# First expert products of a PEER layer: one 512-column matmul for both parts of x, slabs of 256 experts with all 1024 rows

## Chip, cores and metric

The kernel runs on one core of one Trainium2 chip. The metric is the device time of one execution in microseconds. Three executions of the kernel before took 1482.37 (median), 1482.51 and 1480.81 us.

## The reference, cut to what matters

Two transformer blocks follow one another on 256 tokens of width 1024 (float32). The change sits in the last operation, the PEER layer of the second block:

```python
def peer(h, w_q, sub_keys, expert_u, expert_v):      # h: (1, 256, 1024)
    q = einsum('bsd,dq->bsq', h, w_q)                # 8 heads x 2 x 128
    scores = einsum('bshpc,hpnc->bshpn', q, sub_keys)
    top_s, top_i = top_k(scores, 16)
    ...                                              # 256 candidates, the best 16 per head, softmax: gate, best_i
    u = take(expert_u, best_i)                       # expert_u, expert_v: (16384, 1024)
    act = gelu(einsum('td,tkd->tk', x, u), approximate=False)
    v = take(expert_v, best_i)
    return einsum('tk,tkd->td', gate * act, v)
```

The kernel gathers nothing: it computes x times all 16384 rows of expert_u, applies gelu, multiplies by a dense table of gates (zero where an expert wasn't chosen), and multiplies by all of expert_v.

## The kernel before, in words

**Slabs.** All large weights come in 207 slabs of 1 MB (128 partitions x 2048 float32), numbered in order of use. Four slots hold them. For each slab n the sync engine's queue (SP) issues the load once VectorE is done with slab n-4 (`load`, L295 to L300). ScalarE copies the slab to a rounded fp32r high part once TensorE is done with slab n-4 (`hi`, L986 to L992). VectorE subtracts, which gives the low part (`lo`, L1348 to L1353). TensorE takes slab n when both are there (`take`) and signals with `used`. A product of float32 quality is three fp32r matmuls (`mm3`, L417): high x high, high x low, low x high. All matmuls are issued from L412, so rows name them by their tiles.

**Stages of the PEER layer.** Slabs 71 to 78 are query weights, 79 to 142 are expert_u (S_EU, 64 slabs), 143 to 206 are expert_v (S_EV, 64 slabs). In what follows "U slab s" is slab 79+s. Two U slabs make one chunk c of 512 experts: the first holds rows 0 to 511 of the model width for these 512 experts, the second rows 512 to 1023. `feature_half` (L887) runs 4 groups of 128 experts x 4 blocks of 128 rows, three matmuls of 256 tokens each: 48 matmuls per slab, with the weights stationary and x moving. The sums of a chunk fill two PSUM banks (0 and 1 for even c, 2 and 3 for odd c). After the second slab ScalarE applies gelu straight from PSUM to `hidden_out` (L1313 to L1318), SP stores it to HBM (L372 to L376), and TensorE may use the banks for chunk c+2 (L944).

**Side work in the U stage.** VectorE's program is one hand-written sequence. Between its `lo(next(slab))` calls it does the top-k work (`choose`, four calls with six slabs each, L1772), then the keys of the chosen experts (`chosen_keys`), and from U slab 32 on the gate table: 32 gate steps of 16 compares each (`gate_step`, L1899), one or two per slab in turn (`gates_due`, L93). TensorE multiplies what each step made (`gate_step`, L928), into banks 4 to 7, ScalarE copies it (`copy_gates`), and SP stores every four steps (L377). Before the first gate step VectorE waits until ScalarE has copied three transposed selections, the last of which TensorE makes after U slab 31 (L1921, L951, L1327). The order of VectorE around that wait is:

```python
            DVE.wait_ge(*after("choice_copied", 3))
            for n in slab:
                lo(n)
                s = n - S_EU - 4
                for i in range(gates_due(s + 1), gates_due(s + 2)):
                    gate_step(i)
```

**Into the V stage.** SP runs ahead. After the load of slab 142 it issues `load_weighted` for c = 0, 1, 2 (two loads of 512 KB each, hidden values and gates, L383 to L387), then slabs 143 and 144, then the store of hidden chunk 28, slabs 145 and 146, the store of chunk 29, and so on, all in one queue. Their source lines are:

```python
                if n == S_EV - 1:
                    for k in range(2):
                        SP.wait_ge(*after(f"gates_stored{k}", 16 * (S // GATE_T // 2)))
                    for c in range(3):
                        load_weighted(c)
```

VectorE multiplies hidden values by gates (`weigh`, L1914), ScalarE rounds (`weighted_hi`, L1309), VectorE subtracts (`weighted_low`, L1918), and TensorE multiplies with expert_v in matmuls of 512 columns.

Of the kernel before, what the change touches and what calls it, by code (L numbers as in the profile page):

```python
# [6 lines left out]
P = 128  # L7
S = 256
# [134 lines left out]
def program(nc, a, out):  # L143
# [5 lines left out]
    with ctx:  # L149
# [7 lines left out]
        xh = sb("x_hi", [P, KT, S], f32r)  # L157
        xl = sb("x_lo", [P, KT, S], f32r)
# [129 lines left out]
        w_lo = [wl[:], xl[:, 0:EX_A], xl[:, EX_A:2 * EX_A]]  # L288
        hidden_store = nc.dram_tensor("hidden_store", (EX_N, P, EX_A * S), f32).ap()
# [3 lines left out]
        def sync_program():  # L293

            def load(n):  # L295
                name, j = slabs[n]
                if n >= NSLOT:
                    SP.wait_ge(lo_made[n % NSLOT], n // NSLOT)
                src = a[name].rearrange("n p m -> (n p) m")[j * P:j * P + P, :]
                SP.dma_start(raw[:, n % NSLOT, :], src).then_inc(raw_loaded[n % NSLOT], 16)  # L300
# [68 lines left out]
            for n in range(S_PQ + 2, S_END):  # L369
# [39 lines left out]
        def tensor_program():  # L409
# [548 lines left out]
            for c in range(EX_N):  # L958
# [16 lines left out]
                if c == 1:  # L975
                    PE.wait_ge(*after("gate2_diagonal_made", 1))
                    PE.wait_ge(*after("hidden_made", EX_N))
                    for half in range(2):
                        ins = mm(ps[:, half, :], ones[:], carve(1024, TB, 512)[:, half, :])
                    ins.then_inc(sem("gate2_spread"), 1)  # L980

        def scalar_program():
# [3 lines left out]
            def hi(*numbers):  # L986
                for n in numbers:
                    slot = n % NSLOT
                    ACTE.wait_ge(raw_loaded[slot], 16 * (n // NSLOT + 1))
# [320 lines left out]

            for s in range(2 * EX_N):
                c, half = divmod(s, 2)
                if half:  # L1313
                    if c >= 2:
                        ACTE.wait_ge(*after(f"hidden_stored{c % 2}", 16 * (c // 2)))
                    slab_done(ACTE, S_EU + s)
                    ACTE.activation(hidden_out[c % 2], banks(2 * (c % 2), 2).rearrange("p (a t) -> p a t", a=EX_A),  # L1317
                                    ACT.Gelu).then_inc(sem("hidden_made"), 1)  # L1318
# [11 lines left out]
                if s == 2 * EX_N - 3:  # L1330
                    weighted_hi(0)

# [10 lines left out]
        def vector_program():  # L1343
# [427 lines left out]

            def choose(c):  # L1772
# [8 lines left out]
                lo(next(slab))  # L1781
# [4 lines left out]
                lo(next(slab))  # L1786
# [8 lines left out]
                lo(next(slab))  # L1795
# [3 lines left out]
                lo(next(slab))  # L1799
# [14 lines left out]
                lo(next(slab))  # L1814
# [8 lines left out]
                lo(next(slab))  # L1823
# [5 lines left out]
            for _ in range(5):  # L1829
                lo(next(slab))  # L1830
# [15 lines left out]
            lo(next(slab))  # L1846
# [12 lines left out]
            lo(next(slab))  # L1859
# [12 lines left out]
            lo(next(slab))  # L1872

            def chosen_keys(src, m, dst, tb):
# [6 lines left out]
                lo(next(slab))  # L1881
# [8 lines left out]
            lo(next(slab))  # L1890
            chosen_keys(of_i, 0, sa, 1).then_inc(sem("first_keys_made"), 1)
            lo(next(slab))
            V(chosen_keys(of_j, 1, sbb, 0))
            lo(next(slab))
            chosen_keys(of_j, 1, sbb, 1).then_inc(sem("second_keys_made"), 1)
            lo(next(slab))


            def gate_step(i):  # L1899
                n, t0 = i % 2, 8 * i  # L1900
                if i >= 2:
                    DVE.wait_ge(*after("hits_used", 2 * (i - 2) + 2))
                for j in range(8):
# [18 lines left out]
            for n in slab:  # L1922
                lo(n)
# [10 lines left out]
            lo(next(slab))  # L1934
# [103 lines left out]
```

## Time and profile before

| | |
|---|---|
| three executions | 1480.81, 1482.37, 1482.51 us |
| the profiled execution | 1480.88 us, span of its instructions 1479.6 us |
| TensorE busy | 1393.1 us (94%) |
| VectorE busy | 967.1 us (65%) |
| ScalarE busy | 623.9 us (42%) |
| DMA queue of SP | 316 MB, 59.4% of 16 engines |
| mean granted clock of TensorE | 0.965 |

Busy times are sums over the span. A timeline lists each instruction with its start, its duration and the idle time of its engine before it, with what released it. Matmuls overlap in the pipeline, so the time that one costs is the distance between two starts, not its duration. "Landing" of a DMA is the time from its issue to its completion signal.

### The profile page before, as it was taken

The page shows a single profiled execution, that of the slowest core. Times are in us where ns is not written, and L with a number is a line of the kernel's source. Part 1 is how long each engine was busy: PE and PEld are TensorE (multiplying, and loading weights), DVE is VectorE, ACT ScalarE, POOL GpSimd, SP SyncE. Part 2 cuts the span into 40 slices and gives each one's busy share as a digit, 9 for nine tenths or more (in the row PEclk, how much of TensorE's full clock was granted, in tenths as well). Part 3 has the DMA queues.
Part 4 walks back from the last instruction along what each step waited for, and adds up shares of the span by engine and source line. Part 5 has one row for each costly group of instructions (what it writes and reads, how often), then busy time and mean ns, then how long its engine had stood idle before and what let it go on. Part 6 is the DMA issues. An engine that isn't in the chain of part 4 may idle for free.

```text
span 1479.6 us, 19658 instructions
## 1 busy us (share of the span) xinstructions
PE 1393.1 (94%) x8262; PEld 1230.3 (83%) x8262; DVE 967.1 (65%) x1527; ACT 623.9 (42%) x534; POOL 35.1 (2%) x31
## 2 busy tenths in 40 slices
PE   4897968999999999799999999999999999999998
PEld 3786747888888988699999999999997777777776
DVE  4453645888736684748887879899446565655654
ACT  4344434443424853344434444444444434344341
POOL 0010010000002010000000000000000000000000
PEclk9999979999989998899999999999999999999999
DMA  7440316899724311436676748878887777777660
GB/s 292 153 169 3 114 42 273 320 381 377 276 73 185 115 57 58 190 123 214 217 235 225 240 156 270 264 247 256 270 321 279 281 257 271 278 280 277 257 256 29
DMA packets 83239, 317.39 MB, mean 215 GB/s; under 512 B 6096, under 2 KB 40144, under 8 KB 53200
## 3 DMA queue, kind: packets, MB, share of 16 engines
q1 hardware_dynamic: 83152, 316.14, 59.4%
q8 instruction: 65, 1.06, 0.3%
q14 instruction: 22, 0.18, 0.0%
HBM read 281.51 MB, written 34.60 MB: 214 GB/s over the span
## 4 chain that ended last, share of the span: by engine, by line
PE 81%; DVE 11%; ACT 7%; issue 1%; DMA 0%; POOL 0%; ACTq 0%; POOLq 0%
PE psum L412 78%; DVE slab_lo L1352 5%; ACT slab_hi L992 4%; PE psum L415 2%; DVE arena L1914 1%; DVE x_lo L1918 1%; ACT arena L1083 0%; DVE weighted_lo L1918 0%; ACT x_hi L1006 0%; DVE residual L1418 0%; ACT arena L995 0%; DMA arena<-in_mem 0%; DVE arena L1391 0%; DVE arena L1389 0%; ACT x_hi L1309 0%
## 5 line engine op out<-in xcount | busy, mean ns | idle before, releaser
L1352 DVE TENSOR_TENSOR slab_lo<-slab_raw,slab_hi 128x2048 fp32r<-128x2048 f32 x207 | 471.9, 2289 | 284.0 <-ACT slab_hi L992 274.5
L992 ACT ACTIVATE slab_hi<-slab_raw 128x2048 fp32r<-128x2048 f32 x207 | 393.6, 1909 | 273.2 <-PE psum L412 273.2
L412 PE MATMUL psum<-x_hi,slab_hi 128*128 128x256 f32 x1216 | 348.3, 286 | 3.7 <-ACT x_hi L1006 2.7
L412 PE MATMUL psum<-x_lo,slab_hi 128*128 128x256 f32 x1216 | 345.1, 284 | 0.0
L412 PE MATMUL psum<-x_hi,slab_lo 128*128 128x256 f32 x1216 | 345.0, 284 | 0.0
L412 PE MATMUL psum<-slab_hi,x_hi 128*128 128x512 f32 x768 | 311.0, 405 | 31.6 <-DVE slab_lo L1352 11.5
L412 PE MATMUL psum<-slab_lo,x_hi 128*128 128x512 f32 x768 | 304.7, 397 | 0.0
L412 PE MATMUL psum<-slab_hi,x_lo 128*128 128x512 f32 x768 | 304.5, 396 | 0.0
L412 PEld LDWEIGHTS psum<-x_hi,slab_hi 128*128 128x128 f32 x1216 | 234.4, 193 | 4.8 <-issue 3.1
L412 PEld LDWEIGHTS psum<-x_lo,slab_hi 128*128 128x128 f32 x1216 | 234.5, 193 | 0.0
L412 PEld LDWEIGHTS psum<-x_hi,slab_lo 128*128 128x128 f32 x1216 | 234.3, 193 | 0.0
L412 PEld LDWEIGHTS psum<-slab_hi,x_hi 128*128 128x128 f32 x768 | 148.1, 193 | 72.4 <-DVE x_lo L1918 16.1
L412 PEld LDWEIGHTS psum<-slab_hi,x_lo 128*128 128x128 f32 x768 | 147.5, 192 | 31.9
L412 PEld LDWEIGHTS psum<-slab_lo,x_hi 128*128 128x128 f32 x768 | 147.9, 193 | 29.9 <-issue 0.2
L412 PE MATMUL psum<-slab_hi,weighted_hi 128*128 128x512 f32 x280 | 111.7, 399 | 4.9 <-DVE weighted_lo L1918 2.9
L412 PE MATMUL psum<-slab_lo,weighted_hi 128*128 128x512 f32 x280 | 109.9, 392 | 0.0
L412 PE MATMUL psum<-slab_hi,weighted_lo 128*128 128x512 f32 x280 | 109.7, 392 | 0.0
L1906 DVE TENSOR_SCALAR arena<-iota,selected_first_keys,selected_gates 128x128 f32<-128x128 f32 x256 | 87.9, 343 | 0.0
L1317 ACT ACTIVATE arena<-psum 128x1024 f32<-128x1024 f32 x32 | 32.8, 1026 | 127.4 <-PE psum L412 127.4
L412 PEld LDWEIGHTS psum<-slab_hi,weighted_hi 128*128 128x128 f32 x280 | 52.9, 189 | 19.8 <-DVE weighted_lo L1918 7.7
L415 PE MATMUL psum<-ident,arena 128*128 128x128 f32 (+3 forms) x240 | 37.5, 312 | 30.2 <-DVE arena L1371 14.6
L412 PEld LDWEIGHTS psum<-slab_hi,weighted_lo 128*128 128x128 f32 x280 | 53.0, 189 | 11.3
(233 smaller groups left out, 1215.7 us busy)
## 6 DMA issues: line engine op xcount, KB each, us to landing
slab_raw<-in_ex_u SPq DMA_DIRECT2D x64, 1024.0 KB, 5.9
slab_raw<-in_ex_v SPq DMA_DIRECT2D x64, 1024.0 KB, 5.7
arena<-in_w_ada SPq DMA_DIRECT2D x24, 1024.0 KB, 6.9
slab_raw<-in_w_in SPq DMA_DIRECT2D x22, 1024.0 KB, 5.4
slab_raw<-in_w_gu SPq DMA_DIRECT2D x22, 1024.0 KB, 7.2
hidden_store<-arena SPq DMA_DIRECT2D x32, 512.0 KB, 6.9
gates_store<-arena SPq DMA_DIRECT2D x8, 2048.0 KB, 9.7
arena<-hidden_store SPq DMA_DIRECT2D x32, 512.0 KB, 5.8
```

Of the source, the lines that this page charges most:

```text
L412: return PE.matmul(out, lhsT, rhs, start=start, stop=stop)
L415: return PE.transpose(out, in_, ident[0:in_.shape[0], 0:in_.shape[0]])
L992: ACTE.activation(slab_hi[:, slot, :], raw[:, slot, :], ACT.Copy).then_inc(hi_made[slot], 1)
L1317: ACTE.activation(hidden_out[c % 2], banks(2 * (c % 2), 2).rearrange("p (a t) -> p a t", a=EX_A), ACT.Gelu).then_inc(sem("hidden_made"), 1)
L1352: DVE.tensor_tensor(slab_lo[:, slot, :], raw[:, slot, :], slab_hi[:, slot, :].bitcast(f32), ALU.subtract).then_inc(lo_made[slot], 1)
L1906: ins = DVE.tensor_scalar(gated[n][:, j, :], iota[:], sel_a[:, t], sel_g[:, t], ALU.is_equal, ALU.mult)
L1914: DVE.tensor_tensor(w4, w4, gates_in[n], ALU.mult).then_inc(sem("weighted_made"), 1)
L1918: DVE.tensor_tensor(w_lo[c % 3], hidden_in[c % 3], w_hi[c % 3].bitcast(f32), ALU.subtract).then_inc(sem("weighted_lo"), 1)
```

## The change

The two U slabs of a chunk are cut the other way: each slab now holds 256 experts with all 1024 rows. Its load is two DMAs that pick 1 KB pieces (256 float32) out of two of the old slabs. x_hi and x_lo become one tile `x_parts`, so that one matmul of 512 columns multiplies a high block of weights with both parts of x: the left half of a bank collects high x high and, by a second matmul of 256 columns, low x high; the right half collects high x low. After each slab ScalarE copies the right halves to a scratch tile (`hidden_low`), VectorE adds them to the left halves into `hidden_out` (`expert_sum`), and gelu runs in place one chunk later. TensorE reuses a pair of banks every second slab and waits for the sum. The store of hidden chunk c-2 must have landed before the sum of the first slab of chunk c; before, gelu of chunk c waited for it. Before the three first `load_weighted` SP waits for the 60th sum, because the scratch tile lies where they land.

```diff
-        xh = sb("x_hi", [P, KT, S], f32r)
-        xl = sb("x_lo", [P, KT, S], f32r)
+        xx = sb("x_parts", [P, 2, KT, S], f32r)
+        xh, xl = xx[:, 0], xx[:, 1]
...
+        LAST_HIT = 2 * EX_N - 4
+        def hidden_low(s):
+            flat = wf[:] if s < GATE_FROM else zs[:] if s >= LAST_HIT else carve(10240, 1024)
+            return flat[:, (s % 2) * 512:(s % 2) * 512 + 512].rearrange("p (a t) -> p a t", a=2)
...
+                if name == "ex_u":
+                    c, q = divmod(j, 2)
+                    src = a[name].rearrange("n p (k m) -> n p k m", k=4)[:, :, :, q * S:q * S + S]
+                    for half in range(2):
+                        SP.dma_start(raw[:, n % NSLOT, :].rearrange("p (k n) -> p k n", k=KT)[:, 4 * half:4 * half + 4, :], src[2 * c + half]).then_inc(
+                            raw_loaded[n % NSLOT], 16)
...
                 if n == S_EV - 1:
                     for k in range(2):
                         SP.wait_ge(*after(f"gates_stored{k}", 16 * (S // GATE_T // 2)))
+                    SP.wait_ge(*after("hidden_summed", LAST_HIT))
                     for c in range(3):
                         load_weighted(c)
...
+            def expert_half(bank, n):
+                take(n)
+                bh, bl = parts(n % NSLOT, KT, S)
+                for m in range(2):
+                    col = slice(m * P, m * P + P)
+                    for k in range(KT):
+                        mm(ps[:, bank + m, :], bh[:, k, col], xx[:, :, k, :], k == 0, False)
+                        ins = mm(ps[:, bank + m, 0:S], bl[:, k, col], xh[:, k, :], False, k == KT - 1)
+                used(ins, n)
+
             for s in range(2 * EX_N):
-                c, half = divmod(s, 2)
-                if half == 0:
-                    if c < 2:
-                        PE.wait_ge(*after("query_copied", 3 + c))
-                    else:
-                        PE.wait_ge(*after("hidden_made", c - 1))
-                feature_half(2 * (c % 2), S_EU + s, half)
+                if s < 2:
+                    PE.wait_ge(*after("query_copied", 3 + s))
+                else:
+                    PE.wait_ge(*after("hidden_summed", s - 1))
+                expert_half(2 * (s % 2), S_EU + s)
...
+            def hidden_gelu(c):
+                ACTE.wait_ge(*after("hidden_summed", 2 * c + 2))
+                ACTE.activation(hidden_out[c % 2], hidden_out[c % 2], ACT.Gelu).then_inc(sem("hidden_made"), 1)
+
             for s in range(2 * EX_N):
                 c, half = divmod(s, 2)
+                slab_done(ACTE, S_EU + s)
+                if s >= 2:
+                    ACTE.wait_ge(*after("hidden_summed", s - 1))
+                ACTE.activation(hidden_low(s), ps[:, 2 * half:2 * half + 2, S:2 * S], ACT.Copy).then_inc(
+                    sem("hidden_low_copied"), 1)
                 if half:
-                    ...
-                    ACTE.activation(hidden_out[c % 2], banks(2 * (c % 2), 2).rearrange("p (a t) -> p a t", a=EX_A),
-                                    ACT.Gelu).then_inc(sem("hidden_made"), 1)
+                    if c:
+                        hidden_gelu(c - 1)
                 hi(S_EU + s + 4)
...
+            hidden_gelu(EX_N - 1)
...
+            def expert_sum(s):
+                c, q = divmod(s, 2)
+                DVE.wait_ge(*after("hidden_low_copied", s + 1))
+                if q == 0 and c >= 2:
+                    DVE.wait_ge(*after(f"hidden_stored{c % 2}", 16 * (c // 2)))
+                DVE.tensor_tensor(hidden_out[c % 2][:, 2 * q:2 * q + 2, :], ps[:, 2 * q:2 * q + 2, 0:S], hidden_low(s),
+                                  ALU.add).then_inc(sem("hidden_summed"), 1)
+
+            def prepare(n):
+                s = n - S_EU - NSLOT
+                if 0 <= s < 2 * EX_N:
+                    expert_sum(s)
+                lo(n)
```

Every `lo(next(slab))` from slab 73 on becomes `prepare(next(slab))`, and `lo(n)` in the gate loop `prepare(n)`. So the sum of U slab s stands right before the low part of U slab s+4. `hi` waits for both DMAs of a U slab, and the wait at L977 is for all 64 sums.

## Rows read from the trace of the kernel before

**Rows 1.** Windows view: columns are wall, PE, PEld, DVE, ACT, POOL, PEclk, DMA share, GB/s
```profile
640.00:860.00 220.00, 220.00 (x1841) 220.00 (x1841) 166.75 (x479) 96.12 (x66) 0.00 (x0) 1.00 0.64 218
868.61:1038.95 170.34, 170.20 (x1452) 170.16 (x1453) 159.30 (x518) 74.92 (x61) 0.00 (x0) 1.00 0.79 246
1116.62:1474.00 357.38, 347.60 (x1492) 277.83 (x1492) 206.82 (x122) 140.98 (x90) 0.00 (x0) 1.00 0.66 247
```
**Rows 2.** Timeline of PE in the U stage: matmuls 0 and 43 of a row
```profile
799.82 0.28 PE L412 MATMUL psum<-x_hi,slab_lo 128*128 128x256 f32 x1
...
804.98 0.28 PE L412 MATMUL psum<-x_hi,slab_hi 128*128 128x256 f32 x1
```
**Rows 3.** Timeline of PE elsewhere: matmuls 0 and 17 of a row, 512 columns
```profile
459.69 0.39 PE L412 MATMUL psum<-slab_hi,x_hi 128*128 128x512 f32 x1
...
463.54 0.39 PE L412 MATMUL psum<-slab_hi,x_lo 128*128 128x512 f32 x1
```
**Rows 4.** Groups by shape, DVE and ACT: busy us, mean ns
```profile
L1387 DVE TENSOR_TENSOR arena<-psum,columns 128x512 f32<-128x512 f32 x16 | 10.5, 685 | 21.4 <-PE psum L415 21.4
L1648 DVE TENSOR_TENSOR arena<-arena,psum 128x768 f32<-128x768 f32 x4 | 3.8, 950 | 6.0 <-PE psum L412 6.0
L1136 ACT ACTIVATE hidden<-psum 128x512 f32<-128x512 f32 x11 | 6.6, 600 | 36.7 <-PE psum L412 36.7
```
**Rows 5.** Windows view: one choose cycle of 6 slabs, then one gate cycle of 2
```profile
746.90:781.46 34.56, 34.56 (x291) 34.56 (x289) 28.65 (x107) 14.23 (x9) 0.00 (x0) 1.00 0.69 227
941.28:958.15 16.87, 16.87 (x146) 16.87 (x145) 15.37 (x52) 7.48 (x6) 0.00 (x0) 1.00 0.73 238
```
**Rows 6.** Timeline of DVE at its longest gap between two low parts
```profile
751.91 2.27 DVE L1352 TENSOR_TENSOR slab_lo<-slab_raw,slab_hi 128x2048 fp32r<-128x2048 f32 x1
...
758.42 2.29 DVE L1352 TENSOR_TENSOR slab_lo<-slab_raw,slab_hi 128x2048 fp32r<-128x2048 f32 x1 [0.39 <-ACT slab_hi L992]
```
**Rows 7.** Timeline of ACT after U slab 31
```profile
859.66 1.03 ACT L1317 ACTIVATE arena<-psum 128x1024 f32<-128x1024 f32 x1 [3.84 <-PE psum L412]
860.58 1.91 ACT L992 ACTIVATE slab_hi<-slab_raw 128x2048 fp32r<-128x2048 f32 x1
862.38 0.38 ACT L1327 ACTIVATE selected_second_keys<-psum 128x256 f32<-128x256 f32 x1
```
**Rows 8.** Timeline of DVE after U slab 31: low parts of U slabs 34 to 36
```profile
862.79 2.29 DVE L1352 TENSOR_TENSOR slab_lo<-slab_raw,slab_hi 128x2048 fp32r<-128x2048 f32 x1 [9.50 <-ACT selected_second_keys L1327]
868.61 2.29 DVE L1352 TENSOR_TENSOR slab_lo<-slab_raw,slab_hi 128x2048 fp32r<-128x2048 f32 x1
878.06 2.29 DVE L1352 TENSOR_TENSOR slab_lo<-slab_raw,slab_hi 128x2048 fp32r<-128x2048 f32 x1
```
**Rows 9.** Timeline of PE: start of U slab 34
```profile
879.11 0.36 PE L412 MATMUL psum<-x_hi,slab_hi 128*128 128x256 f32 x1
```
**Rows 10.** Timeline of SP before the V stage
```profile
1063.40 0.89 SPq L375 DMA_DIRECT2D hidden_store<-arena  x1
1064.40 0.36 SPq L364 DMA_DIRECT2D arena<-hidden_store  x1
...
1074.55 0.33 SPq L300 DMA_DIRECT2D slab_raw<-in_ex_v  x1
1074.92 0.43 SPq L375 DMA_DIRECT2D hidden_store<-arena  x1
```
**Rows 11.** DMA view, issued between 1071 and 1076 us: x, KB, us to landing
```profile
hidden_store<-arena SPq DMA_DIRECT2D x1, 512.0 KB, 11.6
```
**Rows 12.** DMA view, issued between 690 and 860 us
```profile
hidden_store<-arena SPq DMA_DIRECT2D x15, 512.0 KB, 6.8
```
**Rows 13.** Windows view of 2 us in that burst
```profile
1074.00:1076.00 2.00, 2.00 (x19) 2.00 (x18) 0.52 (x1) 0.88 (x1) 0.00 (x0) 1.00 1.03 420
```
**Rows 14.** Timeline of PE: first matmuls of V chunk 0 and V chunk 1
```profile
1103.66 0.45 PE L412 MATMUL psum<-slab_hi,weighted_hi 128*128 128x512 f32 x1
...
1116.62 0.50 PE L412 MATMUL psum<-slab_hi,x_hi 128*128 128x512 f32 x1 [1.82 <-DVE x_lo L1918]
```
**Rows 15.** DMA issues of the page: stores made of 512 B pieces
```profile
gates_store<-arena SPq DMA_DIRECT2D x8, 2048.0 KB, 9.7
```

More of the change, by code:

```diff
@@ L288, in program, with transfers @@
         w_lo = [wl[:], xl[:, 0:EX_A], xl[:, EX_A:2 * EX_A]]
+        def transfers(n):
+            return sum(32 if S_EU <= m < S_EV else 16 for m in range(n % NSLOT, n + 1, NSLOT))
+        LAST_HIT = 2 * EX_N - 4
+        def hidden_low(s):
+            flat = wf[:] if s < GATE_FROM else zs[:] if s >= LAST_HIT else carve(10240, 1024)
+            return flat[:, (s % 2) * 512:(s % 2) * 512 + 512].rearrange("p (a t) -> p a t", a=2)
         hidden_store = nc.dram_tensor("hidden_store", (EX_N, P, EX_A * S), f32).ap()
@@ L988, in hi @@
                     slot = n % NSLOT
-                    ACTE.wait_ge(raw_loaded[slot], 16 * (n // NSLOT + 1))
+                    ACTE.wait_ge(raw_loaded[slot], transfers(n))
                     if n >= NSLOT:
@@ L1780, in choose @@
                     V(DVE.max_index(U(i16[:, 0:8]), v16[:, 0:8], values))
-                lo(next(slab))
+                prepare(next(slab))
                 for values, v16, i16 in rows[4:8]:
@@ L1785, in choose @@
                     V(DVE.match_replace(values, v16[:, 0:8], values, NEG))
-                lo(next(slab))
+                prepare(next(slab))
                 V.after()
@@ L1794, in choose @@
                     V(DVE.max(v16[:, 8:16], values))
-                lo(next(slab))
+                prepare(next(slab))
                 V.after()
@@ L1798, in choose @@
                     V(DVE.max_index(U(i16[:, 8:16]), v16[:, 8:16], values))
-                lo(next(slab))
+                prepare(next(slab))
                 V.after()
@@ L1813, in choose @@
                     V(DVE.max(v16[:, 0:8], values))
-                lo(next(slab))
+                prepare(next(slab))
                 V.after()
@@ L1822, in choose @@
                     V(DVE.max(v16[:, 8:16], values))
-                lo(next(slab))
+                prepare(next(slab))
                 V.after()
@@ L1829, in vector_program @@
             for _ in range(5):
-                lo(next(slab))
+                prepare(next(slab))
             choose(0)
@@ L1845, in vector_program @@
                 sem("gate_differences_made"), 1)
-            lo(next(slab))
+            prepare(next(slab))
             V.after()
@@ L1858, in vector_program @@
             V(DVE.tensor_tensor(of_j, mid, low_2, ALU.add))
-            lo(next(slab))
+            prepare(next(slab))
             DVE.wait_ge(*after("gate_exp_made", 1))
@@ L1871, in vector_program @@
             shape = [P, PEER_H, TOPK, TOPK]
-            lo(next(slab))
+            prepare(next(slab))
             def chosen_keys(src, m, dst, tb):
@@ L1880, in chosen_keys @@
                 V(DVE.tensor_tensor(key, hit, tfh[:, :, m, :].unsqueeze(3).to_broadcast(shape), ALU.mult))
-                lo(next(slab))
+                prepare(next(slab))
                 for half in (8, 4, 2):
@@ L1889, in vector_program @@
             V(chosen_keys(of_i, 0, sa, 0))
-            lo(next(slab))
+            prepare(next(slab))
             chosen_keys(of_i, 0, sa, 1).then_inc(sem("first_keys_made"), 1)
-            lo(next(slab))
+            prepare(next(slab))
             V(chosen_keys(of_j, 1, sbb, 0))
-            lo(next(slab))
+            prepare(next(slab))
             chosen_keys(of_j, 1, sbb, 1).then_inc(sem("second_keys_made"), 1)
-            lo(next(slab))
+            prepare(next(slab))
             def gate_step(i):
@@ L1902, in gate_step @@
                     DVE.wait_ge(*after("hits_used", 2 * (i - 2) + 2))
+                if i == 1:
+                    DVE.wait_ge(*after("hidden_summed", GATE_FROM))
                 for j in range(8):
@@ L1922, in vector_program @@
             for n in slab:
-                lo(n)
+                prepare(n)
                 s = n - S_EU - 4
@@ L1931, in vector_program @@
                     break
-            lo(next(slab))
+            prepare(next(slab))
             for c in range(EX_N):
```

10 lines of the change are left out of this document (4 added, 6 removed).

## The prediction

> **What bounds the kernel now.** I read the windows first, because the share of busy time (94% for TensorE) says nothing of where a stage is bound. From 640 to 860 us TensorE is busy all the time, VectorE 76% of it; in the gate stretch from 868.6 to 1039 us TensorE is again never idle, but VectorE is busy 159 of 170 us; in the V stage TensorE is at 97% [rows 1]. The granted clock is 1.00, the 2.4 GHz level, in all three, so no clock stands to be won. The U stage is therefore bound by TensorE's issue, with VectorE close behind in its second half. Next the timeline of TensorE, for the distance between starts: 43 matmuls of 256 columns take 5.16 us, 120 ns each [rows 2]; 17 of 512 columns take 3.85 us, 226.5 ns each [rows 3]. 256 more columns cost 106.5 ns, so each matmul costs some 13.4 ns beside its columns. Last the timelines of VectorE, ScalarE and SP, at the three places where the new waits fall: between two low parts, at U slab 31, and at the way into the V stage.
>
> **TensorE's part.** A U slab was 48 x 120 ns = 5.76 us. It becomes 16 x (226.5 + 120) = 5.55 us: the columns are the same, 16 matmuls fewer. That is 0.21 us per slab where TensorE is the bound. What it is worth is read stretch by stretch, since the change adds a sum to VectorE and ties TensorE to it: U slab s may start only when sum s-2 is made, one slab of time after U slab s-2 ended. The trace has no mixed row of 512 and 256 columns and none whose moving operand lies in two pieces; the bounds are 333 ns (both at the column rate) and 360 ns for the pair (no gain at all), and I take 346.5 from the two rows that have these shapes.
>
> A sentence of the skill speaks against the change here: the Trainium skill, "TensorE: Matmul & The Clock Gate", section "Wait — 56ns, not 53.3ns?", puts the fixed cost of a matmul at the full clock at about 2.5 ns beside its columns, for which the whole U stage would gain some 1024 x 2.5 ns = 2.6 us (an estimate from that page) and not 13.7. The trace doesn't agree: it shows 13.4 ns in both shapes [rows 2, 3].
>
> **The prices on the other engines.** The sum reads 128x512 from PSUM; such an operation takes 0.69 us, or some 0.60 us where the next one overlaps its end, as the low parts do (2.29 us long, 2.20 apart) [rows 4, 6]. I take 0.60; the ends are 0.60 and 0.95 (the 768-column row). The copy of the right halves takes 0.60 us on ScalarE [rows 4], which is busy 14.2 of 34.6 us [rows 5] and has the room. Gelu moves, 1.03 us as before [rows 7]. If ScalarE were full, each slab would pay these 0.6 us.
>
> **U slabs 0 to 31.** One choose cycle is six slabs: VectorE works 28.65 of 34.56 us [rows 5]. After: 28.65 + 6 x 0.60 = 32.3 us against 6 x 5.55 = 33.3 us. TensorE stays the bound, narrowly. The longest stretch between two low parts is 6.51 - 0.39 = 6.1 us [rows 6], 6.7 with a sum; a sum may be late by 4 us (a slab less copy and sum), so single long stretches are absorbed, except the first (the same work between the low parts of U slabs 4 and 5, when VectorE comes late out of the queries), where I count 0.6 us. The sum of an even slab also waits for the store of two chunks ago. Gelu now comes 1.9 us after the end of an odd slab; the store follows at once in an otherwise empty queue. Behind a slab load a store lands 6.8 us after issue [rows 12], of which 2.5 us are the slab at 420 GB/s [rows 13]; so alone some 4.7 us. It lands 6.6 us after the slab's end, and VectorE comes to that sum after some 8.6. Cost nothing; cover 2 us. Gain: 32 x 0.21 - 0.6 = 6.2 us.
>
> **U slabs 32 and 33.** VectorE waits for the third selection and now holds sum 30 behind that wait, so TensorE can't start U slab 32. ScalarE starts 0.25 us after slab 31's end (859.4): copy 0.5, gelu 1.0, high part 1.8, selection 0.4: VectorE starts at +3.95 (before: 862.79, +3.4) [rows 7, 8], TensorE at +4.7 instead of about +0.4. VectorE then goes from there to the end of gate step 2 in 878.06 - 862.79 = 15.27 us plus two sums [rows 8], to +20.4; the second half of TensorE's step 2 ends at +21.4, where U slab 34 started at +19.7 before [rows 9]. Cost 1.7 us.
>
> **U slabs 34 to 53.** A cycle of two slabs and three gate steps was 16.87 us with 15.37 us of VectorE [rows 5]. TensorE would need 16.44, VectorE needs 15.37 + 1.2 = 16.6 us: VectorE becomes the bound. Nine cycles gain 9 x 0.27 = 2.4 us, slabs 52 and 53 (one step each) 0.4 us. With a sum of 0.75 us the gain is gone. **U slabs 54 to 59** have no side work: 6 x 0.21 = 1.3 us.
>
> **Into the V stage.** Count from the end of U slab 59. Before, SP issued the three pairs of weighted loads at 1064.40, some 16 us ahead of that point, slab 144 at 1074.55, the store of chunk 28 at 1074.92, and that landed 11.6 us later, at 1086.5 [rows 10, 11]; gelu 30 needed it only at 1092. Now SP waits for sum 59, at +1.45. Behind it stand six 512 KB loads, two slabs and the store of chunk 28: 5.8 MB, 13.7 us at 420 GB/s [rows 13]. With the 3.4 us of fixed time that rows 12 leave (0.4 + 6.8 - 3.75 us of transfer) the store lands at +18.6. Sum 60 waits for it, and so does U slab 62, which would start at +11.1 and starts at +19.3. U slab 63 ends at +30.4. From there to V chunk 1 it was 12.96 us (1116.62 - 1103.66) [rows 14], through ScalarE's high part and VectorE's two low parts; the copy adds 0.5. V chunk 1 starts at +43.8; before, at 1116.62 - (1103.66 - 4 x 5.76) = +36.0. Cost 7.8 us, with the four slabs' gain in it. The V stage then runs as it did: its stalls come from the order of ScalarE and VectorE in each chunk and are not made up. Ends: 1074.92 + 11.6 - 1064.4 = 22.1 us for the same burst with older transfers ahead of it (3.5 us more cost), and 2.9 us of cost if only slab 143 is late (landing +14, and so sum 61, which stands behind its low part).
>
> **DMA.** A U load becomes 1024 pieces of 1 KB. A gates store moves 4096 pieces of 512 B in 9.7 us to landing [rows 15], so 1024 pieces take at most a quarter of it, 2.4 us, if the number of pieces counts, and half of it, 4.9 us, if the bytes do. Between 2.4 and 4.9 I take 3.0, near the bytes' rate in rows 13. A load is issued some 15 us before its use; cost nothing. Without that cover the gate stretch (share 0.79 [rows 1]) would be where it shows.
>
> **Sum.** 6.2 - 1.7 + 2.4 + 0.4 + 1.3 - 7.8 = 0.8 us faster: 1480.1 for the profiled execution of 1480.88 (span 1479.6). That execution is 1.5 us below the median of 1482.37; on the median's scale it is 1481.6. About 0.2%, 3 us, is what a measurement of this kernel can tell from no change.
>
> **Rivals.** (1) **The burst isn't in the way**: the store lands before its 5.2 MB of forerunners are through. Against it: in rows 11 it waited its turn. Then the last term is 2.9, the sum 5.7, the time 1476.7. (2) **VectorE becomes the bound of the whole U stage.** It decides from 0.75 us for a sum (rows 5: (33.3 - 28.65) / 6 and (16.87 - 15.37) / 2). At 0.95 us a choose cycle is 34.35, 1.1 over TensorE's, four times: 4.3 us lost; a gate cycle is 17.27, so 3.6 lost and not 2.4 won. Time 1481.6 + 4.3 + 6.0 = 1491.9. For it: VectorE's work in the gate stretch is 94%; against: its waits release within 0.05 us of ScalarE's end. (3) **The change doesn't save what it says**: the pair stays near 360 ns. Lost are 6.8, 2.4, 1.7 and 0.9 us: 1493.4. By the fixed cost of 2.5 ns as a mechanism of this kernel a slab saves 0.04 us and not 0.21; the same terms shrink to a fifth or less, 1490.9. That is the rule of the page named above, which rows 2 and 3 speak against. (4) **1 KB pieces fill the queues**: at 5.9 us of all 16 engines per slab, twice my value, a gate slab of 8.3 us has 5.9 + 2.7 for its share of a gates store + 0.6: 0.9 us too much, over 20 slabs 18 us: 1499.
>
> **How the numbers follow.** The forecast, within 3 us of no change: 0.38. Rival 1 and a milder burst: 0.24. Rival 2, with the burst's upper end: 0.23. Rival 3: 0.07 (of which 0.02 for the page's value), rival 4: 0.06. Some 0.02 is left for a gain that I don't see. Faster 0.26, within 0.2% 0.38, slower 0.36. The range reaches from rival 1 with a bit of the other ends, 1475.5, to a little short of rival 2's full price, 1490.5.
>
> **What the profile after would show.** 512 and 256 columns in turn, 346 ns a pair, and 5.55 us per slab up to U slab 31; TensorE idle for 4 us before U slab 32; VectorE without idle time in the gate stretch and a cycle of 16.6 us; one stall of about 8 us before U slab 62, released by a sum that waited for the store of chunk 28. I am wrong if that stall is missing, if TensorE waits for sums all through the choose cycles, or if loads of U slabs release ScalarE.

## The result, and the profile after

The changed kernel takes 1489.13 us, the median of 5 runs (1488.25 to 1489.67), against 1481.48 us for the kernel before (5 runs, 1480.81 to 1482.51). The ratio is 1.0045 with an interval of [1.0032, 1.0057]: slower by 7.65 us. The forecast was no change (1481.6); the time lies within the range, just short of its upper end of 1490.5. The profiled execution took 1489.13, its span is 1487.7 us. Page of the kernel after: its first part, then its queue, then the U loads and the stores:

```profile
PE 1388.5 (93%) x7238; PEld 1177.9 (79%) x7238; DVE 1004.5 (68%) x1591; ACT 656.7 (44%) x598; POOL 35.1 (2%) x31
...
q1 hardware_dynamic: 141520, 316.14, 59.8%
...
slab_raw<-in_ex_u SPq DMA_DIRECT2D x128, 512.0 KB, 5.3
...
hidden_store<-arena SPq DMA_DIRECT2D x32, 512.0 KB, 3.1
```

TensorE's share fell from 94% to 93%. U loads in 1 KB pieces land in 5.3 us (median), a store of the hidden values, now alone in the queue, in 3.1 (the forecast had 4.7 for it). None of this says where 8 us went. For that I cut both traces at the same events: ScalarE's first instruction after the end of a slab, which comes 0.25 us behind TensorE (gelu or the high part before [rows 7], the copy of the right halves after).

| stretch | before, us | after, us | change | forecast |
|---|---|---|---|---|
| end of U slab 0 to U slab 31 | 680.68 to 859.66: 178.98 | 680.20 to 856.56: 176.36 | -2.6 | -6.2 (slab 0 among them) |
| U slab 31 to 34 | to 885.21: 25.55 | to 885.80: 29.24 | +3.7 | +1.7, and slab 34's part |
| U slab 34 to 52 | to 1037.01: 151.80 | to 1034.52: 148.72 | -3.1 | -2.4 |
| U slab 52 to 59 | to 1080.88: 43.87 | to 1077.56: 43.04 | -0.8 | -1.7 |
| U slab 59 to start of V chunk 1 | to 1116.62: 35.74 | to 1124.51: 46.95 | +11.2 | +7.8 |
| V chunk 1 to the end | to 1479.6: 362.98 | to 1487.7: 363.2 | +0.2 | 0 |

With the 0.5 us by which slab 0 ended earlier, the changes add up to +8.1 us, the difference of the two spans. Those 0.5 us say nothing: slab 0 ends between 679.3 and 683.2 us in the ten profiles of this study, although the change and the edits leave alone what stands ahead of the U stage, but for the layout of x. So later readings go from the end of U slab 0 to V chunk 1, 435.94 us before and 444.31 after. V chunk 1 after, timeline of TensorE:

```profile
1124.51 0.50 PE L431 MATMUL psum<-slab_hi,x_parts 128*128 128x512 f32 x1 [1.65 <-DVE x_parts L1970]
```

**The pair of matmuls.** Timeline of TensorE, L431, kernel after (the rows that answer to [rows 2, 3]), U slabs 1 and 5:

```profile
681.73 0.40 PE L431 MATMUL psum<-x_parts,slab_hi 128*128 128x512 f32 x1
681.96 0.28 PE L431 MATMUL psum<-x_parts,slab_lo 128*128 128x256 f32 x1
...
684.50 0.40 PE L431 MATMUL psum<-x_parts,slab_hi 128*128 128x512 f32 x1
...
704.33 0.40 PE L431 MATMUL psum<-x_parts,slab_hi 128*128 128x512 f32 x1
...
706.10 0.40 PE L431 MATMUL psum<-x_parts,slab_hi 128*128 128x512 f32 x1
```

Eight pairs in 2.77 us are 346 ns each, the forecast's value; five pairs in 1.77 us are 354. The first pace held up to slab 2, the second in the 28 slabs behind the first stall. ScalarE's timeline shows them as slabs of 5.55 and 5.65 us:

```profile
685.74 0.60 ACT L1348 ACTIVATE weighted<-psum 128x512 f32<-128x512 f32 x1 [3.14 <-PE psum L431]
691.29 0.60 ACT L1348 ACTIVATE weighted<-psum 128x512 f32<-128x512 f32 x1 [3.14 <-PE psum L431]
697.83 0.60 ACT L1348 ACTIVATE weighted<-psum 128x512 f32<-128x512 f32 x1 [4.12 <-PE psum L431]
...
748.71 0.60 ACT L1348 ACTIVATE weighted<-psum 128x512 f32<-128x512 f32 x1 [2.30 <-PE psum L431]
754.35 0.60 ACT L1348 ACTIVATE weighted<-psum 128x512 f32<-128x512 f32 x1 [3.25 <-PE psum L431]
```

28 slabs x 0.1 us = 2.8 us, most of the 3.6 us that are missing in the first stretch.

**The three stalls.** Timeline of TensorE, its matmuls that waited for a sum of VectorE (L1813):

```profile
691.87 0.50 PE L431 MATMUL psum<-x_parts,slab_hi 128*128 128x512 f32 x1 [0.61 <-DVE arena L1813]
...
860.96 0.79 PE L431 MATMUL psum<-x_parts,slab_hi 128*128 128x512 f32 x1 [4.21 <-DVE arena L1813]
...
1098.29 0.80 PE L431 MATMUL psum<-x_parts,slab_hi 128*128 128x512 f32 x1 [9.47 <-DVE arena L1813]
```

They stand before U slabs 3, 32 and 62, where the forecast had 0.6, 4.3 and 8.2 us. It had no price for what comes behind them. Windows view of stretches of 20 us and one of 6 (columns as in [rows 1]):

```profile
860.00:880.00 20.00, 19.05 (x113) 17.19 (x113) 19.79 (x57) 6.81 (x8) 0.00 (x0) 0.84 0.38 130
900.00:920.00 20.00, 20.00 (x139) 18.36 (x138) 20.00 (x60) 9.67 (x10) 0.00 (x0) 1.00 0.93 286
1080.00:1100.00 20.00, 10.53 (x55) 8.90 (x55) 4.75 (x3) 6.75 (x6) 0.00 (x0) 0.79 1.00 386
860.00:866.00 6.00, 5.04 (x15) 4.30 (x16) 5.79 (x16) 0.18 (x1) 0.00 (x0) 0.50 0.27 88
```

The same stretches in the kernel before:

```profile
860.00:880.00 20.00, 17.94 (x150) 17.50 (x149) 17.21 (x51) 9.93 (x9) 0.00 (x0) 1.00 0.42 133
1080.00:1100.00 20.00, 20.00 (x169) 20.00 (x168) 8.01 (x4) 10.35 (x7) 0.00 (x0) 1.00 0.77 280
```

Between the stalls the granted clock is 1.00, the 2.4 GHz level, and before the change it is 1.00 in these two stretches as well. Around the two long stalls it is now 0.84 and 0.79 as a mean over the window; from 860 to 866 us it is 0.50, the 1.2 GHz level. ScalarE's timeline has the slabs' ends (+0.25 us):

```profile
856.56 0.60 ACT L1348 ACTIVATE weighted<-psum 128x512 f32<-128x512 f32 x1 [3.25 <-PE psum L431]
...
869.24 0.60 ACT L1348 ACTIVATE arena<-psum 128x512 f32<-128x512 f32 x1 [9.07 <-PE psum L431]
...
1092.54 1.91 ACT L1020 ACTIVATE slab_hi<-slab_raw 128x2048 fp32r<-128x2048 f32 x1 [8.73 <-DMA slab_raw<-in_ex_v]
...
1105.74 0.60 ACT L1348 ACTIVATE hidden<-psum 128x512 f32<-128x512 f32 x1 [3.07 <-PE psum L431]
```

U slab 32 took 869.24 - 0.25 - 860.96 = 8.0 us, U slab 62 1105.74 - 0.25 - 1098.29 = 7.2 us, where a slab otherwise has 5.55 or 5.65. Between them ScalarE waited 8.73 us for slab 143, which stands in the same burst.

**The way into the V stage.** SP's timeline (the rows that answer to [rows 10]), then VectorE's at sum 60:

```profile
1079.04 0.33 SPq L382 DMA_DIRECT2D arena<-hidden_store  x1
...
1082.36 1.37 SPq L318 DMA_DIRECT2D slab_raw<-in_ex_v  x2
1083.77 1.16 SPq L393 DMA_DIRECT2D hidden_store<-arena  x1
```

```profile
1078.19 0.69 DVE L1813 TENSOR_TENSOR arena<-psum,arena 128x512 f32<-128x512 f32 x1 [1.56 <-ACT arena L1348]
1080.94 2.29 DVE L1387 TENSOR_TENSOR slab_lo<-slab_raw,slab_hi 128x2048 fp32r<-128x2048 f32 x1 [2.05 <-ACT slab_hi L1020]
1097.54 0.69 DVE L1813 TENSOR_TENSOR arena<-psum,hidden 128x512 f32<-128x512 f32 x1 [14.31 <-DMA hidden_store<-arena]
```

SP issued the first weighted load when sum 59 (1078.19) was made, and behind it everything else. The DMA view of the same stretch gives the store of chunk 28, issued at 1083.77, 13.7 us to landing (11.6 before [rows 11]):

```profile
hidden_store<-arena SPq DMA_DIRECT2D x1, 512.0 KB, 13.7
```

It landed at 1097.5. VectorE had stood still for 14.31 us since its low part at 1080.94; sum 60, and through it U slab 62, followed at once. From the end of U slab 59 (1077.56 - 0.25) that is +20.2 us.

**The gate stretch.** Windows view of one gate cycle after, to set beside the second of [rows 5]:

```profile
897.00:913.44 16.44, 16.44 (x114) 15.00 (x113) 16.44 (x54) 8.38 (x9) 0.00 (x0) 1.00 0.95 289
```

Both engines are busy all the time, so the distance between starts has to tell. VectorE's first low part of a cycle, in the first of nine cycles and behind the last:

```profile
877.27 2.29 DVE L1387 TENSOR_TENSOR slab_lo<-slab_raw,slab_hi 128x2048 fp32r<-128x2048 f32 x1
...
1025.19 2.55 DVE L1387 TENSOR_TENSOR slab_lo<-slab_raw,slab_hi 128x2048 fp32r<-128x2048 f32 x1
```

That is 147.92 us, 16.44 a cycle. TensorE's nine cycles, U slab 34 to 52, take 148.72, 16.52 each. Neither waits for the other here: TensorE's only waits for a sum are the three stalls, and VectorE, once it has the selections at 860.21, waits next at 1042.49. So by these rows TensorE still sets the pace of the stretch, by 0.08 us a cycle. Its pairs have both paces here: 14 pairs take 4.95 us in U slab 36 and 4.85 in U slab 37, and every third slab is a slow one. The nine cycles take 148.72 us in all seven profiles that have the wide matmul and single sums. Whoever reads VectorE's recorded durations here should take the starts instead: the compares of a gate step are recorded 0.32 and 0.38 us long, and a pair starts every 0.45; and the low part above is recorded 2.29 us long at first and 2.55 at the end, with the same distance between cycles.

### The profile page after: what moved, and what is told of

Its sections match the earlier page's. It is cut to its first block, busy times and chain, and to the rows that moved or that the text cites. A ratio compares the mean times of both kernels' runs of the same rounds, so it can differ in the third digit from the quotient of the medians.

```text
span 1487.7 us, 17864 instructions
## 1 busy us (share of the span) xinstructions
PE 1388.5 (93%) x7238; PEld 1177.9 (79%) x7238; DVE 1004.5 (68%) x1591; ACT 656.7 (44%) x598; POOL 35.1 (2%) x31
## 3 DMA queue, kind: packets, MB, share of 16 engines
q1 hardware_dynamic: 141520, 316.14, 59.8%
## 4 chain that ended last, share of the span: by engine, by line
PE 78%; DVE 11%; ACT 7%; issue 1%; DMA 1%; SPq 0%; POOL 0%; ACTq 0%; DVEq 0%; POOLq 0%
PE psum L431 76%; DVE slab_lo L1387 6%; ACT slab_hi L1020 4%; PE psum L434 2%; DVE arena L1966 1%; DMA hidden_store<-arena 1%; DVE x_parts L1970 1%; ACT arena L1111 0%; DVE weighted_lo L1970 0%; ACT x_parts L1034 0%; DVE residual L1453 0%; ACT arena L1023 0%; DVE arena L1426 0%; DMA arena<-in_mem 0%; DVE arena L1424 0%
## 5 line engine op out<-in xcount | busy, mean ns | idle before, releaser
L431 PE MATMUL psum<-slab_hi,x_parts 128*128 128x512 f32 x1536 | 500.8, 402 | 31.4 <-DVE slab_lo L1387 11.5
L431 PE MATMUL psum<-x_parts,slab_hi 128*128 128x512 f32 (+1 forms) x1408 | 439.7, 372 | 17.9 <-DVE arena L1813 14.3
L431 PEld LDWEIGHTS psum<-slab_hi,x_parts 128*128 128x128 f32 x1536 | 296.4, 193 | 105.1 <-DVE x_parts L1970 15.9
L431 PE MATMUL psum<-x_parts,slab_lo 128*128 128x256 f32 x1216 | 343.7, 283 | 0.0
L431 PEld LDWEIGHTS psum<-x_parts,slab_hi 128*128 128x128 f32 x1408 | 255.9, 192 | 66.0 <-DVE arena L1813 15.2
L431 PE MATMUL psum<-slab_lo,x_parts 128*128 128x512 f32 x768 | 305.8, 398 | 0.0
L431 PEld LDWEIGHTS psum<-x_parts,slab_lo 128*128 128x128 f32 x1216 | 233.0, 192 | 0.0
L431 PEld LDWEIGHTS psum<-slab_lo,x_parts 128*128 128x128 f32 x768 | 148.6, 193 | 30.0 <-issue 0.2
L431 PE MATMUL psum<-slab_hi,weighted_hi 128*128 128x512 f32 x280 | 111.1, 397 | 5.3 <-DVE weighted_lo L1970 3.0
L431 PE MATMUL psum<-slab_hi,weighted_lo 128*128 128x512 f32 x280 | 109.1, 390 | 0.0
L431 PE MATMUL psum<-slab_lo,weighted_hi 128*128 128x512 f32 x280 | 109.1, 390 | 0.0
L431 PEld LDWEIGHTS psum<-slab_hi,weighted_hi 128*128 128x128 f32 x280 | 52.6, 188 | 20.4 <-DVE weighted_lo L1970 7.7
L434 PE MATMUL psum<-ident,arena 128*128 128x128 f32 (+3 forms) x240 | 37.7, 313 | 31.0 <-DVE arena L1406 14.5
L431 PEld LDWEIGHTS psum<-slab_hi,weighted_lo 128*128 128x128 f32 x280 | 52.6, 188 | 11.2
L431 PEld LDWEIGHTS psum<-slab_lo,weighted_hi 128*128 128x128 f32 x280 | 52.6, 188 | 10.3
L431 PE MATMUL psum<-arena 128*128 128x128 f32 (+10 forms) x300 | 51.8, 327 | 5.6 <-DVE arena L1520 1.3
## 6 DMA issues: line engine op xcount, KB each, us to landing
gates_store<-arena SPq DMA_DIRECT2D x8, 2048.0 KB, 10.7
```

Source lines behind the costliest of these rows:

```text
L431: return PE.matmul(out, lhsT, rhs, start=start, stop=stop)
L434: return PE.transpose(out, in_, ident[0:in_.shape[0], 0:in_.shape[0]])
```

## The experiments

**Is it the order in SP's queue?** The wait for sum 59 and the three pairs of loads go behind the store of chunk 28:

```diff
                 if n == S_EV - 1:
...
-                    SP.wait_ge(*after("hidden_summed", LAST_HIT))
-                    for c in range(3):
-                        load_weighted(c)
+                if n == S_EV + 1:
+                    SP.wait_ge(*after("hidden_summed", LAST_HIT))
+                    for c in range(3):
+                        load_weighted(c)
```

> Edit: SP issues slabs 143 and 144 and the store of hidden chunk 28 ahead of the wait for sum 59 and of the three weighted loads. Theory Q (the wait stands in SP's queue ahead of things that others need sooner; what counts is the bytes between the wait and the landing of that store): the 9.5 us stall before U slab 62 is gone, V chunk 1 starts about 36 us after the end of U slab 59 (the changed kernel: 47.2), time about 1478. Rival D (VectorE's sums are what cost; the stall only shows where): TensorE's lost time comes back in other stalls and the time stays above 1485.

Measured: 1479.30 us, ratio 0.999 [0.9974, 1.0007] to the kernel before. The stall before U slab 62 is gone. Timelines of ScalarE, at the ends of U slabs 59 to 61, and of TensorE, at V chunk 0 (all lines of this kernel one higher):

```profile
1076.68 0.60 ACT L1349 ACTIVATE arena<-psum 128x512 f32<-128x512 f32 x1 [3.15 <-PE psum L432]
...
1082.23 0.60 ACT L1349 ACTIVATE hidden<-psum 128x512 f32<-128x512 f32 x1 [2.20 <-PE psum L432]
...
1087.78 0.60 ACT L1349 ACTIVATE hidden<-psum 128x512 f32<-128x512 f32 x1 [3.15 <-PE psum L432]
```

```profile
1101.73 0.76 PE L432 MATMUL psum<-slab_hi,weighted_hi 128*128 128x512 f32 x1 [2.90 <-issue]
```

U slab 59 to V chunk 1 takes 37.7 us instead of 46.95: 9.2 of the 11.2 us are the queue's order and what followed from it. The rest is the next item of the same queue: sum 62 now waited 4.16 us for the store of chunk 29, which stands behind the weighted loads. V chunk 0's low part stands behind that sum in VectorE's order (sum at 1097.61, low part at 1100.41), and TensorE idled for 2.90 us before V chunk 0.

**How much of the burst must go?** Only the third pair of loads waits (it alone lands where the scratch tile of sums 32 to 59 lies; the first two pairs never needed the wait that the change gave them); the first two are issued at the old place, ahead of the wait, and the two slabs and the store still stand behind it:

```diff
-                    SP.wait_ge(*after("hidden_summed", LAST_HIT))
                     for c in range(3):
+                        if c == 2:
+                            SP.wait_ge(*after("hidden_summed", LAST_HIT))
                         load_weighted(c)
```

> Edit: only the third weighted load waits for sum 59; the first two pairs go ahead of it. Theory Q in size: 3.7 MB instead of 5.8 MB stand from the wait to the end of the store of chunk 28, so it lands 5 us earlier (some 14 to 15 us after the end of U slab 59, not 20.2); a stall of about 3 to 4 us is left before U slab 62, V chunk 1 starts at about +40, time about 1481 to 1482. Rival: if the first-issued transfer's fixed time and not the bytes sets it, the stall stays at 9.5 us and the time at 1489.

Measured: 1482.23 us, 1.001 [0.9997, 1.0022]. Timeline of TensorE:

```profile
1092.23 0.80 PE L432 MATMUL psum<-x_parts,slab_hi 128*128 128x512 f32 x1 [3.97 <-DVE arena L1814]
```

2 MB less behind the wait shorten the stall by 9.47 - 3.97 = 5.5 us and the way into the V stage by 4.6 (42.3 us). At 386 GB/s the 2.1 MB are 5.4 us: the bytes behind the wait set the stall, as this theory had it, and not the fixed time of the first transfer.

**Is the pair at 353 ns a matter of x's layout?** The two parts of x lie side by side for each block, so that the 512 columns are one piece:

```diff
-        xx = sb("x_parts", [P, 2, KT, S], f32r)
-        xh, xl = xx[:, 0], xx[:, 1]
+        xx = sb("x_parts", [P, KT, 2, S], f32r)
+        xh, xl = xx[:, :, 0], xx[:, :, 1]
...
-                        mm(ps[:, bank + m, :], bh[:, k, col], xx[:, :, k, :], k == 0, False)
+                        mm(ps[:, bank + m, :], bh[:, k, col], xx[:, k].rearrange("p a t -> p (a t)"), k == 0, False)
```

> Edit: x_parts is laid out so that the 512 moving columns of a matmul are one contiguous run per partition instead of two of 256. Most slabs of the changed kernel run at 353 ns a pair of matmuls, some at 346.5. Theory P (two pieces of moving data cost the 7 ns): all slabs at 346.5, U slabs of 5.55 us, time 3 to 4 us lower, about 1485.5. Rival S (the 7 ns come from how a slab's row starts or from the order of shapes): the same mix of 346.5 and 353, time 1489.

Measured: 1488.01 us, 1.004 [1.0021, 1.0058], with a stall of 9.67 us before U slab 62 and both paces in the U slabs as before. The layout is not the cause.

**Does the wide matmul save anything?** The slab order, the sums and the waits of the change stay; the 512 columns are two matmuls of 256 again:

```diff
-                        mm(ps[:, bank + m, :], bh[:, k, col], xx[:, :, k, :], k == 0, False)
+                        mm(ps[:, bank + m, 0:S], bh[:, k, col], xh[:, k, :], k == 0, False)
+                        mm(ps[:, bank + m, S:2 * S], bh[:, k, col], xl[:, k, :], False, False)
```

> Edit: the 512-column matmul is split again into two of 256 columns, into the left and the right half of the bank; everything else of the change stays. It prices the one saving alone. Theory (the saving is real at 6.6 to 13.4 ns a pair): U slabs 5.76 us, the gate cycle bound by TensorE at 16.87 us, U slabs 0 to 31 3 us longer, gate stretch 2.7 us longer, the rest 1 us: about 1496. Rival (the 512-column matmul saves nothing where it matters, since VectorE and the queue set the time): 1489, unchanged.

Measured: 1499.43 us, 1.0119 [1.0099, 1.014]. Slabs are 5.76 us and the gate cycle 16.87 again, as before the change. Timeline of ScalarE:

```profile
717.81 0.60 ACT L1349 ACTIVATE weighted<-psum 128x512 f32<-128x512 f32 x1 [2.42 <-PE psum L431]
723.57 0.60 ACT L1349 ACTIVATE weighted<-psum 128x512 f32<-128x512 f32 x1 [3.36 <-PE psum L431]
```

The two long stalls stay, at 4.21 and 8.28 us; the one before U slab 3 is gone. Against the changed kernel the time is 10.3 us more, but not all of that stands where the edit does: from the end of U slab 0 to V chunk 1 it takes 451.08 us, 6.8 more than the changed kernel in its first profile and 10.6 more than in its second (below). So the saving that the change is made of is real, 7 to 11 us, and rival 3 is out.

**Nothing behind the wait.** Two pairs of loads at the old place with no wait at all; the wait and the third pair behind the stores of chunks 28 and 29:

```diff
-                    SP.wait_ge(*after("hidden_summed", LAST_HIT))
-                    for c in range(3):
+                    for c in range(2):
                         load_weighted(c)
+                if n == S_EV + 3:
+                    SP.wait_ge(*after("hidden_summed", LAST_HIT))
+                    load_weighted(2)
```

> Edit: the first two weighted loads go without a wait (their buffers do not overlap the scratch tile), the third waits for sum 59 and stands behind slabs 143 to 146 and the stores of chunks 28 and 29. Theory Q: nothing that is needed sooner stands behind a wait any more. The 4.2 us that sum 62 waited for the store of chunk 29 with the slabs first (and the 2.9 us before V chunk 0) go too; V chunk 1 starts about 36 us after the end of U slab 59 (slabs first: 38.0; changed kernel: 47.2), time 1.5 to 2 us below slabs first, about 1477.5. Rival: the loads are bandwidth, and the same bytes delay something else: 1479 to 1480.

Measured: 1475.64 us, 0.9964 [0.995, 0.9979], faster than both kernels. U slab 59 to V chunk 1 is 35.4 us (before 35.74), and no matmul of a U slab behind the 32nd waits for a sum. Timeline of TensorE, V chunk 0:

```profile
1098.52 0.47 PE L433 MATMUL psum<-slab_hi,weighted_hi 128*128 128x512 f32 x1 [0.45 <-issue]
```

**What does the other stall cost?** On top of that, two sums are made earlier in VectorE's program: sum 30 ahead of the wait for the selections, sum 1 at the start of the second choose call.

```diff
-                if 0 <= s < 2 * EX_N:
+                if 0 <= s < 2 * EX_N and s not in (1, 30):
                     expert_sum(s)
...
+                if c == 1:
+                    expert_sum(1)
...
+            expert_sum(30)
             DVE.wait_ge(*after("choice_copied", 3))
```

> Edit: as the run before, and sum 30 stands ahead of VectorE's wait for the selections, sum 1 at the start of the second choose instead of at its second gap. Theory V (after U slab 31 VectorE is the bound, so TensorE's idle 4.2 us before U slab 32 cost next to nothing): the 4.2 us stall of TensorE vanishes, U slab 34 starts only some 0.6 us earlier; the 0.6 us stall before U slab 3 vanishes; time 1.2 us lower, about 1476.5. Rival T (TensorE's idle time is the cost): 4.8 us and the cold clock lower, about 1472.

Measured: 1474.66 us, 0.9954 [0.9936, 0.9971], the best version of the study; its interval overlaps with that of the run before it, so I read the worth of the edit from the traces. Timeline of ScalarE, ends of U slabs 31, 32 and 34:

```profile
855.00 0.60 ACT L1350 ACTIVATE weighted<-psum 128x512 f32<-128x512 f32 x1 [3.15 <-PE psum L433]
...
860.77 0.60 ACT L1350 ACTIVATE arena<-psum 128x512 f32<-128x512 f32 x1 [2.15 <-PE psum L433]
...
882.06 0.60 ACT L1350 ACTIVATE arena<-psum 128x512 f32<-128x512 f32 x1 [4.05 <-PE psum L433]
```

U slab 32 takes 5.77 us, and U slab 31 to 34 takes 27.06 us; without the early sums it was 29.40. So 2.3 us of the stall reach the end. That lies between the two expectations for this stall, 0.6 us and its full 4.2 with the clock on top. TensorE still waits for VectorE, now in the first gate step (2.07 us), as the first theory has it, and the clock is lowered behind that wait too, but for a shorter time (timeline, then windows view):

```profile
862.80 1.16 PE L433 MATMUL psum<-arena,hidden 128*128 128x128 f32 x8 [2.07 <-DVE arena L1962]
```

```profile
864.00:868.00 4.00, 3.39 (x13) 3.17 (x14) 4.00 (x9) 1.03 (x1) 0.00 (x0) 0.57 0.43 147
```

**How near is VectorE to the bound?** In U slabs 6 to 53 each sum is made twice into the same place (on top of the first experiment):

```diff
+                if 6 <= s < 54:
+                    V(DVE.tensor_tensor(hidden_out[c % 2][:, 2 * q:2 * q + 2, :], ps[:, 2 * q:2 * q + 2, 0:S], hidden_low(s),
+                                        ALU.add))
+                    V.after()
```

> Edit: on top of e1_slabs_first every sum of U slabs 6 to 53 is done twice (some 0.7 us more of VectorE per slab). Theory V: VectorE is within 0.2 us per slab of the bound in the choose cycles and past it in the gate cycles: a choose cycle of six slabs goes from 33.3 to about 36.4 us, a gate cycle of two from 16.57 to about 18.0 us; time some 25 us above e1, about 1504. Rival: if TensorE had held both, the choose cycle would stay at 33.3 and the gate cycle go to about 17.0: 1483.

Measured, one execution: 1501.66 us. A choose cycle of six slabs takes 35.0 and then 36.1 us instead of 33.3, the nine gate cycles (U slab 34 to 52) 160.72 us, 17.86 each instead of 16.5. The timeline of VectorE shows the price of a sum, 0.75 us where another follows that must wait for it and 0.61 ahead of a low part:

```profile
904.69 0.72 DVE L1815 TENSOR_TENSOR arena<-psum,arena 128x512 f32<-128x512 f32 x1
905.44 0.69 DVE L1818 TENSOR_TENSOR arena<-psum,arena 128x512 f32<-128x512 f32 x1
906.05 2.28 DVE L1388 TENSOR_TENSOR slab_lo<-slab_raw,slab_hi 128x2048 fp32r<-128x2048 f32 x1
```

**Is the slow pace of the pair a property of the kernel?** The changed kernel once more, with no edit.

> No edit: the changed kernel once more, for a second profile. Theory S (the 353 or 346.5 ns of a pair of matmuls is a state that a row of matmuls falls into at its start, not a property of the kernel): the slabs may run at either, and may differ from the first profile slab for slab. Rival: the same slabs at the same speed as in the first profile. The stall before U slab 62 is 9.5 us again under both.

Measured, one execution: 1484.13 us, span 1482.7. Timeline of ScalarE:

```profile
696.83 0.60 ACT L1348 ACTIVATE weighted<-psum 128x512 f32<-128x512 f32 x1 [4.02 <-PE psum L431]
702.38 0.60 ACT L1348 ACTIVATE weighted<-psum 128x512 f32<-128x512 f32 x1 [0.77 <-PE psum L431]
...
741.21 0.60 ACT L1348 ACTIVATE weighted<-psum 128x512 f32<-128x512 f32 x1 [3.15 <-PE psum L431]
746.75 0.60 ACT L1348 ACTIVATE weighted<-psum 128x512 f32<-128x512 f32 x1 [2.20 <-PE psum L431]
```

Here the U slabs behind the first stall, up to the 23rd, run at 5.55 us, and slabs 0 to 31 take 173.9 us instead of 176.4. Same program, other pace: it differs between executions. The stalls are where they were, 0.61, 4.21 and 8.73 us. U slab 32 has the same stall ahead of it but takes 7.2 us instead of 8.0, so U slab 31 to 34 takes 28.4 us; 60 to 62 takes 22.0 (22.5 in the first profile). From the end of U slab 0 to V chunk 1 that is 440.51 us, 3.8 less than in the first profile.

This execution lies 4.1 us under the lowest of the five on which the result rests, and inside the range of the 14 executions of the kernel before that ran beside it (1478.68 to 1486.97). That the change slows the kernel is borne out by the kernel with x laid out in one piece (1.004, seven executions, the same stalls and paces); how much, 7.65 us or less, depends on the executions.

## Why the prediction was wrong

Most of the forecast is in the profile at the place that it named: the three stalls, their releasers, loads that never release ScalarE in the U stage, a V stage that moves as one block. One thing is not: VectorE did not become the bound of the gate stretch. The signs of all terms were right; the sizes were not, and they leave the profiled sum 8.9 us off (+8.1 instead of -0.8). What it had at nothing was the clock behind its own stalls. Windows view of the kernel before, from the first weighted load [rows 10] to the landing of the store [rows 11], for the first of the sizes:

```profile
1064.40:1086.00 21.60, 21.60 (x182) 21.60 (x181) 9.13 (x4) 8.69 (x6) 0.00 (x0) 1.00 0.99 377
```

- **"Into the V stage", 7.8 us: the step that failed most.** It is 11.2. The store landed at +20.2 us and not at +18.6: 5.8 MB at the 386 GB/s of the window from 1080 us take 15.0 us, and the forecast took 420 GB/s from a window of 2 us, 13.7. That is 1.3 of the 1.6. The trace of the kernel before had the better number, 377 GB/s over the whole burst (the line above). Another 1.65 us are U slab 62 itself, 7.2 us instead of 5.55, at a lowered clock behind 9.5 us of waiting; the forecast said that "no clock stands to be won" and never asked what its own stalls would do to it. The range had room for this, since its upper end took 3.5 us more here, for older transfers ahead of the burst. That 1489.13 still lies inside the range is in part luck: its upper end was reasoned from rival 2, VectorE as the bound of the U stage, and what filled it was this burst, the clock and the pair's pace.
- **"U slabs 32 and 33", 1.7 us.** It came to 3.7 (2.8 in the second profile, 28.4 us against 25.55). The stall was 4.21 us as forecast. I then let VectorE carry the rest of the way to U slab 34, but TensorE needed 8.0 us for U slab 32 and became the late one. With sum 30 ahead of the wait the stretch took 27.06 us, 1.5 more than before, near the 1.7 that the forecast had for VectorE alone; the 2.2 us on top of that here are TensorE's stall and its lowered clock.
- **"U slabs 0 to 31", 6.2 us of gain, and 54 to 59, 1.3 (with 52 and 53 1.7).** They gave 2.6 and 0.8. The first stall was 0.61 us, as said. The pair was put at 346.5 ns from two pure rows; mixed, it has that pace or 353 ns. With the better one the first stretch gives 5.1 us (173.9 against 178.98), close to the forecast for 31 of its 32 slabs.
- **"U slabs 34 to 53", 2.4 + 0.4 us of gain.** 3.1 up to U slab 52. VectorE's cycle is 16.44 us and not 16.6, and TensorE's 16.52, so VectorE did not become the bound. A sum cost the 0.60 us that was taken (0.61 in the rows of the second-sum experiment), so the rest of the cycle is 15.2 us by its starts, and 15.37 was busy time as recorded [rows 5].
- **The rivals.** Rival 1 (the burst isn't in the way) is refuted for this kernel. Its time, 1476.7, is near the 1475.64 of the kernel with nothing behind the wait, but by luck: the way into the V stage costs -0.3 us there (35.4 against 35.74) where the rival had 2.9, and the U slabs gained less than forecast. Rival 2's mechanism isn't there, yet its margin is: a second sum makes VectorE the bound at once. Its place as the slow case was filled by the burst. Rival 3 is refuted by the kernel with three matmuls, whose U stage is 6.8 to 10.6 us longer than with the change. By the page value of the Trainium skill ("TensorE: Matmul & The Clock Gate", section "Wait — 56ns, not 53.3ns?") it would be 2.6, an estimate; these runs don't agree with it. Rival 4 is refuted: the queue's share is 59.8% after and 59.4% before, with U loads in 1 KB pieces that land in 5.3 us.

So the balance, from the end of U slab 0 to V chunk 1, is this. The new slab order, sums and waits, with three matmuls as before, cost 15.1 us (451.08 against 435.94): 4.2 behind the wait for the selections, 10.7 at the way into the V stage. The wide matmul takes back 6.8 of them in one profile and 10.6 in the other, by the pair's pace and by how long the clock stays down. What isn't settled is what sets that pace. In the traces it changed at a stall or after other matmuls (transposes, gate steps), but some stalls left it as it was; x's layout is excluded.

## What to carry to other kernels

When an edit adds a wait to an issuing queue, count the bytes behind it, at the rate of a window as long as the burst: here the kernel stood still for the last transfer among them, not for the one that needed the wait, and reordering those lines turned 0.45% slower into 0.4% faster. Price a forecast stall at its length and at the slab behind it, here 1.6 to 2.7 us more for stalls of 4 to 10 us. Work that must be done early belongs ahead of an in-order engine's wait, even where the engine itself has time to spare.

## What the runs showed of the hardware

- A lowered clock follows a stall of 4.2 us as well as one of 9.5 (granted 0.84 and 0.79 in the windows around them, where the kernel before has 1.00; one U slab of 8.0 and 7.2 us). Behind the same stall of 4.21 us U slab 32 took 7.2 us in three profiles and 8.0 to 8.3 in three others. The stall of 0.61 us before U slab 3 had no such effect: the slab behind it ended 5.71 us after its start at 691.87. In between, waits of 2.07 and 0.65 us close together were followed by 0.57 over 4 us in the kernel with early sums; waits of 1.41 and 0.65 us at the same place of the kernel before were not (1.00).
- Matmuls of 512 and 256 columns in turn have two paces, 346 and 354 ns a pair, at a granted clock of 1.00. The pace held over many slabs where nothing stood between them, changed from slab to slab among gate steps, and was different in two executions of the same program.
- The burst of weighted loads and slabs moved 386 GB/s over 20 us, against 420 in a window of 2 us of the burst before [rows 13], which over its whole 21.6 us moved 377: the short window overstated what the long burst got.
